# The matrix-memory outputs of a hybrid encoder layer, turned in 32 x 32 blocks on VectorE and put in place by 64 small DMAs

## The reference

```
h  = recurrence over chunks of 64 tokens (q, k, v, gates)     # per head: 256 tokens x 256
h  = rms_norm(h, g_hnorm).reshape(tokens, 2048) * sigmoid(zo)
merged = sigmoid(gate_a) * (y_a @ p_a) + sigmoid(gate_b) * (h @ p_b)
x = x + merged @ w_out          # then cross attention, then the conv-GLU FFN
```

## Time and profile before

| | |
|---|---|
| median of three runs | 1748.78 us |
| profiled execution, own time | 1747.07 us |
| its span | 1745.3 us |
| TensorE busy | 1739.6 us (100% of the span) |
| VectorE busy | 1117.8 us (64%) |
| ScalarE busy | 937.8 us (54%) |
| GpSimd busy | 9.9 us (1%) |
| granted TensorE clock | 1.000 |

### The profile page before, as it was taken

One profiled execution on the slowest core, in us unless ns is written; L12 is line 12 of the kernel. 1 busy time (PEld: TensorE's weight loads), 2 busy tenths in 40 slices (PEclk: granted clock), 3 DMA queues, 4 the chain that ended last, 5 costly groups with the idle time before them and its releaser, 6 DMA issues.

```text
span 1745.3 us, 26005 instructions
## 1 busy us (share of the span) xinstructions
PE 1739.6 (100%) x8742; PEld 1481.7 (85%) x8742; DVE 1117.8 (64%) x1555; ACT 937.8 (54%) x1273; POOL 9.9 (1%) x22
## 2 busy tenths in 40 slices
PE   9999999999999999999999999999999999999999
PEld 7888888888888888888888888888888888888887
DVE  6888876667755454545565666766777666755554
ACT  7765556667754444444654565555555555544443
POOL 0000000000000000000000000000000000000000
PEclk9999999999999999999999999999999999999999
DMA  8555454576756555556755456565565555655554
GB/s 320 192 172 177 170 169 158 170 163 168 183 181 194 192 192 186 193 189 241 284 185 183 145 168 190 184 192 192 192 192 182 191 183 189 190 195 192 192 192 157
DMA packets 91237, 330.79 MB, mean 190 GB/s; under 512 B 10256, under 2 KB 10512, under 8 KB 90160
## 3 DMA queue, kind: packets, MB, share of 16 engines
q1 hardware_dynamic: 89712, 321.96, 55.8%
q0 software_dynamic: 1472, 8.12, 2.8%
HBM read 326.83 MB, written 2.10 MB: 188 GB/s over the span
## 4 chain that ended last, share of the span: by engine, by line
PE 99%; DMA 0%; DVE 0%; SPq 0%; ACT 0%; issue 0%
PE ps L350 22%; PE ps L331 14%; PE ps L333 14%; PE ps L332 14%; PE ps L358 11%; PE ps L746 4%; PE ps L745 4%; PE ps L744 4%; PE ps L461 1%; PE ps L460 1%; PE ps L459 1%; PE ps L504 1%; PE ps L503 1%; PE ps L616 0%; PE ps L518 0%; PE ps L511 0%
## 5 line engine op out<-in xcount | busy, mean ns | idle before, releaser
L1316 DVE TENSOR_TENSOR w_lo<-w_raw,w_hi 128x1024 fp32r<-128x1024 f32 x598 | 729.3, 1224 | 576.9 <-ACT w_hi L792 575.8
L792 ACT ACTIVATE w_hi<-w_raw 128x1024 fp32r<-128x1024 f32 x598 | 628.9, 1058 | 652.4 <-PE ps L333 311.5
L350 PE MATMUL ps<-u,w_hi 128*128 128x512 f32 x1664 | 422.3, 393 | 0.0
L350 PEld LDWEIGHTS ps<-u,w_hi 128*128 128x128 f32 x1664 | 298.1, 189 | 52.2
L331 PE MATMUL ps<-w_hi,u 128*128 128x512 f32 x608 | 240.8, 396 | 0.6 <-DVE w_lo L1348 0.6
L358 PEld LDWEIGHTS ps<-u,w_lo 128*128 128x128 f32 x1664 | 226.9, 190 | 16.4
L333 PE MATMUL ps<-w_hi,u 128*128 128x512 f32 x608 | 237.1, 390 | 0.0
L332 PE MATMUL ps<-w_lo,u 128*128 128x512 f32 x608 | 236.9, 390 | 0.0
L358 PE MATMUL ps<-u,w_lo 128*128 128x256 f32 x1664 | 231.9, 282 | 0.0
L331 PEld LDWEIGHTS ps<-w_hi,u 128*128 128x128 f32 x608 | 114.3, 188 | 24.2 <-DVE u L1343 1.0
L333 PEld LDWEIGHTS ps<-w_hi,u 128*128 128x128 f32 x608 | 114.2, 188 | 24.3
(11 more groups left out here) (344 smaller groups left out, 1918.0 us busy)
## 6 DMA issues: line engine op xcount, KB each, us to landing
w_raw<-in_stream SPq DMA_DIRECT2D x600, 512.0 KB, 3.4
x_tok<-in_x SPq DMA_DIRECT2D x2, 1024.0 KB, 8.6
mem_raw<-in_mem_by_feature POOLq DMA_DIRECT2D x2, 1024.0 KB, 6.8
x_tok<-in_x POOLq DMA_DIRECT2D x2, 1024.0 KB, 7.4
mem_tok<-in_mem POOLq DMA_DIRECT2D x2, 1024.0 KB, 14.1
out<-x_tok SPq DMA_DIRECT2D x8, 256.0 KB, 3.3
x_t<-in_x_t SPq DMA_DIRECT2D x7, 256.0 KB, 5.0
w_raw<-in_stream SPq DMA_DIRECT2D x4, 256.0 KB, 4.7
```

The costliest lines, as they stand in the source:

```text
L350: mm = pe.matmul(ps[:, bank + m, :], w_hi[:, s, lo:lo + P], act[:, kc, :, :].rearrange("p h t -> p (h t)"), start=(kc == 0), stop=(kc == K ...
L792: act.activation(w_hi[:, s, :], w_raw[:, s, :], ACT.Copy).then_inc(hi_made, 1)
L1316: TTo(w_lo[:, s, :], w_raw[:, s, :], w_hi[:, s, :].bitcast(F32), ALU.subtract).then_inc(lo_made, 1)
```

## The change

TensorE's eight transposes a pass go. In their place, between its splits 6 and 7 of a pass, VectorE turns `hn` in eight instructions of 128 x 128. Each turns the sixteen 32 x 32 blocks of its tile in place: inside a block the transpose is complete, but the blocks still stand at the row of blocks they came from. They go to `y_turned`, in SBUF. GpSimd's queue then moves the blocks to the right partitions with 16 DMAs a pass (one for each source and target group of 32 partitions), each of 32 partitions x 8 pieces x 32 elements: 32 KB in pieces of 128 bytes. The targets are `y_first` in the first pass and parts of `qk` no longer needed in the others. ScalarE and VectorE form the two parts of `y_b` from there, from SBUF, one pass later than before: for j-1 at the end of pass j, and for the last pass in the first merge pass, which is therefore written out before the loop. The row spreads are issued one pass ahead of the block moves on the same queue. The other waits in the diff guard buffers that the transposes' order guarded before.

```diff
+            def move_blocks(j):
+                pool.wait_ge(sem("yb_tok"), 8 * j + 8)
+                if j > 1:
+                    pool.wait_ge(sem("yb_hi"), 4 * j - 4)
+                for a in range(4):
+                    for b in range(4):
+                        pool.dma_start(moved(j)[32 * b:32 * b + 32, :, 32 * a:32 * a + 32],
+                                       turned(j)[32 * a:32 * a + 32, :, 32 * b:32 * b + 32]
+                                       ).then_inc(sem(f"yb_moved{j % 2}"), 16)
+
+            spread_rows(0)
+            spread_rows(1)
+            for j in range(NBLK):
+                if j + 2 < NBLK:
+                    spread_rows(j + 2)
+                move_blocks(j)
...
@@ TensorE, mlstm_pass
+                if j:
+                    pe.wait_ge(sem("ml_hn"), 4 * j)
...
-                pe.wait_ge(sem("yb_tok"), 4 * j + 4)
-                for i in range(2):
-                    for half in range(2):
-                        for t in range(TT):
-                            mm = pe.transpose(ps[:, ATT + 2 + i, half * T + t * P:half * T + (t + 1) * P],
-                                              hn[:, i, t, half * P:(half + 1) * P], ident)
-                    mm.then_inc(sem("yb_T"), 1)
...
@@ ScalarE
+            def output_high(j):
+                act.wait_ge(sem(f"yb_moved{j % 2}"), 256 * (j // 2) + 256)
+                for k in range(4 * j, 4 * j + 4):
+                    act.activation(y_b[:, k, 0, :], outputs(j)[:, k % 4, :], ACT.Copy, scale=dcol("g_hnorm", k)
+                                   ).then_inc(sem("yb_hi"), 1)
...
                 split(pos, 7)
-                for i in range(2):
-                    act.wait_ge(sem("yb_T"), 2 * j + (i + 1))
-                    for half in range(2):
-                        n = 2 * i + half
-                        act.activation(y_b[:, bass.ds(4 * j + n, 1), 0, :],
...
+                if j:
+                    output_high(j - 1)
...
@@ VectorE, mlstm_pass
                 split(pos, 6)
+                dve.wait_ge(sem("yb_tok"), 8 * j + 4)
+                for i in range(2):
+                    for t in range(TT):
+                        for half in range(2):
+                            ins = dve.transpose(turned(j)[:, 4 * i + 2 * half + t, :],
+                                                hn[:, i, t, half * P:(half + 1) * P])
+                        ins.then_inc(sem("yb_tok"), 1)
                 split(pos, 7)
                 if j < NBLK - 1:
                     triangles(j + 1)
...
+                if j:
+                    output_low(j - 1)
```

More of the change, by code:

```diff
@@ L137, in build @@
                     [("y_a", [P, KC, 2, T], F32R), ("y_b", [P, KC, 2, T], F32R)],
+                    [("yf_pad", [P, KC * 2 * T + 24 * T], F32), ("y_first", [P, 4, T], F32)],
+                    [("yt_pad", [P, KC * 2 * T], F32), ("y_turned", [P, KC, 2, T], F32)],
                     [("rb_pad", [P, 8192], F32), ("qa_t", [P, LC, 2, T], F32R), ("kv_t", [P, LC, 2, T], F32R)],
@@ L143, in build @@
                     [("h_ff", [P, FC, T], F32)])
-        y_a, y_b, qa_t, kv_t, mem_t = rb["y_a"], rb["y_b"], rb["qa_t"], rb["kv_t"], rb["mem_t"]
+        y_a, y_b, y_first, y_turned, qa_t, kv_t, mem_t = (rb[n] for n in ("y_a", "y_b", "y_first", "y_turned", "qa_t", "kv_t", "mem_t"))
         mem_tok, mem_raw, ck, cv, cq, c_sq, c_p, c_pt, h_ff = (
@@ L190, in build, with turned, outputs, moved @@
         r_x0, eps_x0 = tiny[:, 62:64], tiny[:, 24:26]
+        def turned(j):
+            return y_turned[:, 4 * j:4 * j + 2, :, :].rearrange("p k h (t d) -> p (k h t) d", t=TT)
+        def outputs(j):
+            if j:
+                lo = 8 if j == 2 else 0
+                return qk[:, lo:lo + 4, :]
+            return y_first[:]
+        def moved(j):
+            return outputs(j).rearrange("p k (t d) -> p (k t) d", t=TT)
         def x0_part(kc):
@@ L292, in _, with spread_rows @@
             pool.wait_ge(sem("mla_T"), 3 * PAIRS)
-            for j in range(NBLK):
+            def spread_rows(j):
                 if j:
@@ L1054, in mlstm_pass @@
             def mlstm_pass(pos, j, bank):
+                if j:
+                    act.wait_ge(sem("yb_tok"), 8 * j - 4)
                 sigmoid_block(bank)
@@ L1097, in _, with merge_pass @@
                 mlstm_pass(Pos(G_ML + j * KPB), j, GEMM + 2 * (1 - j % 2))
+            act.wait_ge(sem("yb_tok"), 8 * NBLK - 4)
             sigmoid_block(GEMM + 2)
-            def merge_pass(pos, it, last):
-                for c in range(2 * KPB):
+            def merge_pass(pos, it, first, last):
+                for c in range(KPB):
+                    split(pos, c)
+                if first:
+                    output_high(NBLK - 1)
+                for c in range(KPB, 2 * KPB):
                     split(pos, c)
@@ L1122, in merge_pass @@
                     sigmoid_block(ATT + 2)
-            with act.Fori(0, NBLK - 1) as j:
-                merge_pass(Pos(G_MERGE, j, 4 * KPB), j, False)
-            merge_pass(Pos(G_MERGE + 4 * KPB * (NBLK - 1)), NBLK - 1, True)
+            merge_pass(Pos(G_MERGE), 0, True, False)
+            with act.Fori(0, NBLK - 2) as j:
+                merge_pass(Pos(G_MERGE + 4 * KPB, j, 4 * KPB), j + 1, False, False)
+            merge_pass(Pos(G_MERGE + 4 * KPB * (NBLK - 1)), NBLK - 1, False, True)
             for c in range(3, KPB):
@@ L1616, in exponents, with output_low @@
                        ALU.min).then_inc(sem("ml_arg"), 1)
+            def output_low(j):
+                dve.wait_ge(sem("yb_hi"), 4 * j + 4)
+                for k in range(4 * j, 4 * j + 4):
+                    STT(y_b[:, k, 1, :], outputs(j)[:, k % 4, :], dcol("g_hnorm", k), y_b[:, k, 0, :].bitcast(F32),
+                        ALU.mult, ALU.subtract).then_inc(sem("yb_lo"), 1)
             def triangles(j):
@@ L1693, in merge_pass @@
                 for t in range(TT):
-                    TTo(mg_a[:, t, :], ps[:, GEMM + t, :], sig[:, t, :], ALU.mult).then_inc(sem("mga"), 1)
+                    TTo(mg_a[:, t, :], ps[:, GEMM + t, :], sig[:, t, :], ALU.mult).then_inc(sem("mg_read"), 1)
+                if first:
+                    output_low(NBLK - 1)
                 for c in range(KPB, 3 * KPB):
@@ L1698, in merge_pass @@
                 for t in range(TT):
-                    TTo(mg[:, t, :], ps[:, ATT + t, :], sgb[:, t, :], ALU.mult).then_inc(sem("mgb_read"), 1)
-                dve.wait_ge(sem("mgb_read"), TT * it + TT)
-                dve.wait_ge(sem("mga"), TT * it + TT)
+                    TTo(mg[:, t, :], ps[:, ATT + t, :], sgb[:, t, :], ALU.mult).then_inc(sem("mg_read"), 1)
+                dve.wait_ge(sem("mg_read"), 2 * TT * it + 2 * TT)
                 TTo(mg[:], mg[:], mg_a[:], ALU.add).then_inc(sem("mg_made"), 1)
@@ L1717, in merge_pass @@
                         split(pos, c)
-            with dve.Fori(0, NBLK - 1) as j:
-                merge_pass(Pos(G_MERGE, j, 4 * KPB), j, False)
-            merge_pass(Pos(G_MERGE + 4 * KPB * (NBLK - 1)), NBLK - 1, True)
+            merge_pass(Pos(G_MERGE), 0, True, False)
+            with dve.Fori(0, NBLK - 2) as j:
+                merge_pass(Pos(G_MERGE + 4 * KPB, j, 4 * KPB), j + 1, False, False)
+            merge_pass(Pos(G_MERGE + 4 * KPB * (NBLK - 1)), NBLK - 1, False, True)
             def x1_add(n):
```

## The result

The changed kernel takes 1753.56 us (median of 13 runs, 1751.03 to 1755.15); the kernel before, on the same chip, 1748.59 (13 runs, 1747.53 to 1749.87). The ratio is 1.0028, 95% interval 1.0019 to 1.0036: 5 us slower. The profiled execution is one of the two slowest of the 13 (both 1755.15 us), with a span of 1753.4. That of the kernel before (1747.07) was faster than any of its 13. So the account of the traces, +8.1 us of span, is an account of an upper case.

What follows compares the result with a forecast made beforehand. TensorE was taken to bound the kernel, with a 0.36 us margin on the chain feeding it; -3.6 + (0.88 + 2.5) + (0.88 + 1.6) = +2.3 us on the 1748.78 median gave 1751.1 us, range 1745.0 to 1760.0.

Steps and rivals of the forecast that it cites:

- slower by more: Whole kernel: slower by more than 0.2% (3.5 us), the heavy cases and the forecast's upper part; chance 0.37.
- if TensorE waits elsewhere: Sign of being wrong: TensorE waits other than at the weighted values of passes 2 and 3, forecast 3.4 and 2.5 us.
- TensorE's transposes, -3.6: TensorE: removing eight transposes a pass saves 0.90 us a pass, 3.6 us in four passes.
- The chain, 0.88 a pass: ScalarE and VectorE up to L1638: 0.54 + 0.34 = 0.88 us of TensorE wait in each of passes 2 and 3.
- What sticks out is 0.34 us: VectorE before split 7: eight transposes at 0.23 us, 1.84 us, exceed its 1.50 us idle gap by 0.34.
- Without anything else L1638 would be 0.54 us late: Chain to the weighted values: TensorE arrives 0.90 us earlier, the margin is 0.36, so L1638 is 0.54 late.
- The moves, d = 2.8, of which 2.5 and 1.6 reach TensorE: DMA engines: block moves delay ScalarE's weights by d = 16 x 0.175 = 2.8 us; 2.5 reach TensorE in pass 2, 1.6 in pass 3.
- The hidden parts (0.3 and 1.2): Parts of the moves' 2.8 us delay hidden by slack: 0.3 us for pass 2's wait, 1.2 us for pass 3's.
- ScalarE's wait for weights in pass 1 ending near 425.5: Sign: ScalarE's wait for weights in pass 1 ends near 425.5 us instead of 422.97.
- GB/s well below 354: Sign: DMA rate between 420 and 425 us falls well below 354 GB/s.
- d = 1.5 us: Lower bound of the moves' weight delay, giving -0.3 us, 1748.5; rival of chain alone or light moves, chance 0.25.
- everything hidden: Rival: TensorE's 3.6 us come off in full, 1745.2 us; chance 0.11.

Runs made afterwards that it cites:

- experiment 1: Changed kernel without its block moves, y_b formed from four other tiles of qk (result not the reference's); 1748.67 us, ratio to the kernel before 1.0001.
- experiment 5: Changed kernel with early row spreads and without its block moves (result not the reference's); 1745.22 us, ratio to the kernel before 0.9979.
- experiment 11: Changed kernel with row spreads ahead of the mLSTM passes and y_b formed two passes later, off the chain; 1743.77 us, ratio to the kernel before 0.9974.
- experiment 4: Changed kernel with the row spreads for passes 1 to 3 issued ahead of the mLSTM passes into own tiles, moves unchanged; 1745.07 us, ratio 0.9982.
- experiment 3: Changed kernel with each pass's block moves held back until TensorE has left the fifth chunk of the next pass; 1753.11 us.
- experiment 10: Changed kernel with TensorE's weighted values placed behind chunk 4 of their pass instead of chunk 3; 1752.19 us.
- experiment 8: Changed kernel with source and target of the moves laid out by blocks, pieces of 1 KB instead of 128 bytes; 1752.18 us, ratio 1.0021.
- experiment 2: Kernel before, TensorE's transposes kept, with 16 added moves of 128-byte pieces in each of passes 0 and 1; 1754.55 us, ratio 1.0037.
- experiment 6: Kernel before with early row spreads, all eight issued together at 365 us because an old wait was left in; 1765.22 us, ratio 1.0095.
- experiment 9: Changed kernel with y_b formed two passes later, between splits 3 and 4, instead of on the chain behind split 7; 1752.59 us.

## Why the prediction was right, and where it was not

It gave 1751.1 us, 2.5 below the result, and its range of 15 us held that easily. Two waits were forecast at the weighted values of passes 2 and 3, behind L1680, and there they are; the direction and the cause, late weights on a chain with little margin, were right. Two things were not. The size: the change is +5.0 us of medians where +2.3 was forecast. That is 0.28% (0.19 to 0.36): more than the 0.2% up to which the prediction gave 0.52, and in its class "slower by more", 0.37. The place: TensorE also waits at the scores of pass 2, which the prediction named as a sign of being wrong ("if TensorE waits elsewhere"). It had followed the chain to L1638 only. The same late chain makes `v_st`, which the scores need, so this wait is the first part of the same lateness and no further cost.

The sizes are read best from TensorE's starts, since a late start also holds the overlap with the matmul before, which the idle time leaves out (single executions, us; "scores" and "values" are their first products, "merge" the first product of the merge):

| | values, pass 1 | scores, pass 2 | values, pass 2 | scores, pass 3 | values, pass 3 | merge |
|---|---|---|---|---|---|---|
| before | 421.51 | 438.22 | 447.71 | 464.37 | 473.86 | 487.72 |
| changed | 420.58 | 437.36 | 450.93 | 468.34 | 481.12 | 495.83 |
| experiment 1 (no moves) | 420.89 | 436.69 | 448.54 | 465.98 | 476.48 | 489.66 |
| experiment 5 (early spreads, no moves) | 420.72 | 436.52 | 446.57 | 462.44 | 472.49 | 485.69 |
| experiment 11 (no such wait) | 421.15 | 436.95 | 446.44 | 462.20 | 471.69 | 484.76 |

- *TensorE's transposes, -3.6.* Right: from the values of pass 1 to the scores of pass 2 it takes 16.71 us before and 15.80 in experiment 11, 0.91 less, where 0.90 was forecast.
- *The chain, 0.88 a pass.* Its first part was right, its second failed. From scores to values experiment 5 takes 10.05 us against 9.49 without a wait: 0.56 late, where 0.54 was forecast. "What sticks out is 0.34 us" failed: the transposes take 0.199 us from start to start ((411.68 - 410.09) / 8), not 0.23, and nothing of them sticks out. From the release of split 4 by TensorE to the end of L1680 the chain takes 20.62 us in experiment 4 (426.03 to 446.65), 20.67 before.
- *Starved weights without the moves, 0.* This term was missing. "Without anything else L1638 would be 0.54 us late" took the weights' arrival for fixed. From scores to values experiment 1 takes 11.85 us in pass 2 and 10.50 in pass 3, that is 1.80 and 0.45 more than experiment 5, and the two differ only in the spreads. The spreads start when VectorE has read the last ones (L1651), not with TensorE, so a TensorE that runs earlier asks for weights inside the starved stretch. That it is the earlier asking, rather than variation of the transfers, is argued; the 424.1 was seen twice (experiments 1 and 3).
- *The moves, d = 2.8, of which 2.5 and 1.6 reach TensorE.* The size of d was right: counted from pass 0, split 3's weight and the squares are both 2.75 us later than in experiment 1. The hidden parts (0.3 and 1.2) failed. From the values of pass 1 to those of pass 2 the changed kernel takes 30.35 us, experiment 1 27.65: 2.70 arrive, since the starved weights had used up the slack. In pass 3, from scores to values, it is 12.78 against 10.50: 2.28 arrive. There d is no smaller than that: counted from the values of pass 2, split 3's weight comes 2.25 us later than in experiment 1 (456.68 - 450.93 against 452.04 - 448.54).
- *The clock, absent from the sum.* From the values of pass 2 to the scores of pass 3 the changed kernel takes 17.41 us, experiment 11 15.76; from the values of pass 3 to the merge 14.71 and 13.07. That is 1.65 + 1.64 = 3.3 us. Some 0.2 of them come with any wait (experiment 5, clock at 1.00: 15.87 and 13.20), so the slower matmuls cost 3.1. The busy times differ by more, 1740.3 - 1736.3 = 4.0, and are no measure of the clock: experiment 10, whose clock stayed at 1.00 behind six waits, is busy for 1738.4.

Together, for the span: the transposes -3.6, the starts late by 0.98 at the scores of pass 2 (16.78 - 15.80) and by 4.08 and 3.29 at the values (13.57 and 12.78 - 9.49), and what follows the waits +3.3: +8.0 of the measured +8.1. The forecast of +2.3 was 5.8 short in this execution: what follows the waits 3.3, the starved weights 2.25 and the moves 0.2 + 0.7 more than in the sum, the chain 0.6 less. So a part that was too dear hid some of one that was missing. Over the medians it was 2.7 short, as the two profiled executions are a fast one before and a slow one after.

Of the other signs that were named: *ScalarE's wait for weights in pass 1 ending near 425.5*: 426.50 (and a third one, for split 4, until 429.19). *GB/s well below 354*: 228. *`yb_moved` never waited for*: right. GpSimd's transfers cost 0.58 us of issue, not 0.53:

```profile
L321 POOL DMA_DIRECT2D y_first<-y_turned x16: 582/583/617, 412.0 to 420.7; - x16
L1716 DVE STREAM_TRANSPOSE y_turned<-hn x32: 266/268/304, 410.1 to 498.0; 128x128 f32<-128x128 f32 x32
```

Of the two rules that were weighed, the first (the Trainium skill, VectorE: DVE Perf Modes, "The three transpose paths") gives 311 ns for bf16; here, in fp32, one takes 268 ns from start to end and 199 from start to start in a row of eight. Its estimate of 1.0 us sticking out did not come true. The second (the Trainium skill, DMA: Bandwidth & Descriptors, "Why small descriptors are slow (HBM only)") holds that moves within SBUF don't suffer from short pieces; its 78% is for a remote transfer of 1 MB. The estimate from it, d = 1.5 us, is not what the trace shows: the weights beside the moves came 2.75 us later. In pieces of 1 KB it was 1.3 us, so what their neighbours suffer may well depend on the length (experiment 8, single executions).

The rival "everything hidden" at 1745.2 is what experiment 4 reaches, by moving what the moves collided with.

## What to carry to other kernels

Work taken from the engine that sets the time only counts if what feeds it is early enough: look for the narrowest margin between two engines (here 0.36 us in a chain of 20.67), and for what it rests on, a DMA stream as much as instructions. Small side transfers are free or dear by what stands beside them on the DMA engines: the same 64 moves cost 4.9 us with the row spreads among them and nothing that these runs can tell without. Of two disturbers that collide, the one that is free to run elsewhere is the one to move; here it was the older one.

## What was not expected of the hardware

- TensorE's granted clock fell to the 1.2 GHz level after some waits inside a stretch at 2.4 GHz: after 3.81 and 3.14 us (changed kernel), 2.21 (experiment 1), 2.50 (experiment 2), 16.6 (experiment 6), 3.95 (experiment 8) and 2.24 (experiment 9). It stayed at 1.00 after 2.01 and 1.77 (experiment 3), 1.92 and 1.58 (experiment 10) and all shorter ones. In experiment 9 it fell to 0.50 (440 to 442 us) after one of 1.97 as well, which no wait of the same length elsewhere did; why is open. In the changed kernel 7.0 us of waits for `w_low` thus brought 3.1 of slower matmuls.
- 16 moves of 32 KB in pieces of 128 bytes landed after 10.6 and 10.0 us at the median in passes 0 and 1, behind the spreads, and after 3.8 in passes 2 and 3 of the same execution. With the spreads away (experiment 4) those of pass 0 took 3.9.
